# A two-block transformer kernel: the first normalisation by token tiles, wide and narrow matmuls in runs of sixteen, and another order in the mLSTM

## What is computed

```python
# first block, after its four mixers and their gates
mixed = jnp.sum(gates * y, axis=2) @ w_mix_out[l]
x = layer_norm(DEEPNORM_ALPHA * x + mixed, ln_mix_g[l], ln_mix_b[l])   # the first normalisation, "x1"
xa = cross_attention(x, mem_n, xattn_q[l], xattn_k[l], xattn_v[l], xattn_o[l])
x = layer_norm(DEEPNORM_ALPHA * x + xa, ln_x_g[l], ln_x_b[l])          # "x2"
ff = conv_ffn(x, ffn_in[l], ...); x = layer_norm(DEEPNORM_ALPHA * x + ff, ...)

# second block
y_m = mlstm_mixer(q_m, k_m, v_m, o_m, i_m, f_m, conv_w, conv_b, gate_b, mh_g)  # four heads
y_a = dilated_attention(q_a, k_a, v_a, rel_bias)
y = jnp.concatenate([y_m, y_a], axis=-1) @ w_out[l]; x = layer_norm_2(...)
y = memory_cross_attention(x, mem, xq, xk, xv, xo);  x = layer_norm_2(...)     # "x4", "x5"
y = (jax.nn.silu(x @ w1) * (x @ w3)) @ w2;           x = layer_norm_2(...)
```

## Time and profile before

| | |
|---|---|
| median of three runs | 3334.51 us |
| the profiled execution | 3333.03 us |
| its span, first to last instruction | 3331.1 us |
| PE busy | 3271.8 us (98%) |
| DVE busy | 1998.8 us (60%) |
| ACT busy | 1351.2 us (41%) |
| mean granted clock of PE | 0.993 of full speed |
| 16 DMA engines, mean rate | 191 GB/s |

### The profile page before, as it was taken

The page is one execution under the profiler, slowest core; times in us unless marked ns, Lnnn a source line. Parts: engine busy times, 40 slices in busy tenths (PEclk is TensorE's granted clock), DMA queues, the critical chain, the costliest instruction groups (busy, mean ns, idle before and its releaser), DMA issues.

```text
span 3331.1 us, 43422 instructions
## 1 busy us (share of the span) xinstructions
PE 3271.8 (98%) x18557; PEld 2850.6 (86%) x18557; DVE 1998.8 (60%) x1622; ACT 1351.2 (41%) x898; POOL 0.2 (0%) x4
## 2 busy tenths in 40 slices
PE   8999999999989999999999999999999999999998
PEld 8988888887878888888888889799998988888886
DVE  6455666757677666675565675774456644444556
ACT  4333555433335444443333433343333444444332
POOL 0000000000000000000000000000000000000000
PEclk9999999999999999999999999999999999999999
DMA  7744456678536555555646455655545555555553
GB/s 259 218 153 164 173 190 227 216 246 298 165 118 207 197 176 181 197 191 197 217 162 207 157 172 187 208 203 173 169 152 202 193 186 189 189 176 196 195 189 139
DMA packets 309424, 635.60 MB, mean 191 GB/s; under 512 B 10888, under 2 KB 16820, under 8 KB 307124
## 3 DMA queue, kind: packets, MB, share of 16 engines
q1 hardware_dynamic: 296080, 587.50, 52.3%
q10 hardware_dynamic: 13220, 46.25, 3.8%
HBM read 618.51 MB, written 15.20 MB: 190 GB/s over the span
## 4 chain that ended last, share of the span: by engine, by line
PE 89%; DVE 6%; ACT 2%; issue 2%; DMA 1%; ACTq 0%; SPq 0%; DVEq 0%
PE ps L961 40%; PE ps L1026 34%; PE ps L956 14%; ACT whi L570 1%; DVE wlo L1487 1%; PE ps L1030 1%; DMA wraw<-in_w_in 1%; DVE l_a L2148 1%; DVE m_t L1540 0%; DVE alt_l L1540 0%; DVE tok L1697 0%; DVE tok L1702 0%; DVE tok L1540 0%; DVE tok L2325 0%; DVE tok L2324 0%
## 5 line engine op out<-in xcount | busy, mean ns | idle before, releaser
L1487 DVE TENSOR_TENSOR wlo<-wraw,whi 128x2048 fp32r<-128x2048 f32 x549 | 1244.8, 2279 | 756.1 <-ACT whi L570 746.9
L570 ACT ACTIVATE whi<-wraw 128x2048 fp32r<-128x2048 f32 x549 | 1041.9, 1906 | 1424.2 <-PE ps L961 637.7
L1026 PE MATMUL ps<-act_hl,whi 128*128 128x512 f32 (+1 forms) x2976 | 787.4, 384 | 0.0
L961 PE MATMUL ps<-whi,act_hl 128*128 128x512 f32 x2128 | 661.8, 392 | 0.7 <-DVE wlo L1487 0.7
L1026 PEld LDWEIGHTS ps<-act_hl,whi 128*128 128x128 f32 x2976 | 502.3, 188 | 62.6
L1026 PEld LDWEIGHTS ps<-act_hl,wlo 128*128 128x128 f32 x2832 | 438.5, 188 | 57.7
L961 PEld LDWEIGHTS ps<-whi,act_hl 128*128 128x128 f32 x2128 | 396.3, 188 | 83.4 <-issue 1.9
L1026 PE MATMUL ps<-act_hl,wlo 128*128 128x256 f32 x2832 | 463.0, 281 | 0.0
L956 PE MATMUL ps<-act_hl,whi 128*128 128x256 f32 (+1 forms) x2400 | 441.0, 286 | 5.4 <-DVE wlo L1540 4.1
L961 PE MATMUL ps<-wlo,act_hl 128*128 128x512 f32 x1064 | 414.4, 389 | 0.0
L956 PEld LDWEIGHTS ps<-act_hl,whi 128*128 128x128 f32 (+1 forms) x2400 | 376.6, 193 | 8.0 <-issue 5.5
(11 more groups left out here) (322 smaller groups left out, 2443.1 us busy)
## 6 DMA issues: line engine op xcount, KB each, us to landing
wraw<-in_w_in SPq DMA_DIRECT2D x156, 1024.0 KB, 5.2
wraw<-in_w SPq DMA_DIRECT2D x132, 1024.0 KB, 5.2
wraw<-in_ffn_in SPq DMA_DIRECT2D x88, 1024.0 KB, 5.0
wraw<-in_ffn_out SPq DMA_DIRECT2D x44, 1024.0 KB, 5.1
wraw<-in_w_branch SPq DMA_DIRECT2D x16, 1024.0 KB, 5.2
wraw<-in_w_mix_out SPq DMA_DIRECT2D x16, 1024.0 KB, 5.5
wraw<-in_w_out SPq DMA_DIRECT2D x16, 1024.0 KB, 5.4
wraw<-in_xk SPq DMA_DIRECT2D x16, 1024.0 KB, 5.2
```

Of the source, the lines that this page charges most:

```text
L570: act.activation(whi[:, slot, k, c], wraw[:, slot, k, c], ACT.Copy).then_inc(hi_done, 1)
L961: ins = pe.matmul(o, x, wk, start=first and n == 0, stop=stop and n == 2, skip_group_check=True)
L1026: return pe.matmul(o, left, right, start=start, stop=stop, skip_group_check=True)
L1487: dve.tensor_tensor(wlo[:, slot, k, c], wraw[:, slot, k, c], whi[:, slot, k, c].bitcast(F32), ALU.subtract).then_inc(lo_done, 1)
```

## The change

1. `double`: PE waits for the high part of the unit alone, does the sixteen wide matmuls of all four chunks, waits for the low part, and does the sixteen narrow ones. Before, the two kinds alternated in fours.
2. x1 joins the normalisations by token tiles. The last of the mixing product's four columns is made by `last_column` (until now written out for x5 alone), the nine matmuls on constants go, and `gate_apart` makes the queries in two passes: its first pass takes the first token tile with the high weights, its second the second tile and the low weights. Its result is two halves side by side, so that ACT copies one of them out of PSUM first and DVE then adds the other one to it, where DVE copied before. ACT's work on units is redistributed: `hi(13)`, three inside `norm_apart`, `hi(3)`, that copy, `hi(1)`. DVE takes the last quarter's residual from `x_again` tile by tile, and the second tile's sum is put ahead of the scaling of the first tile's last quarter.
3. mLSTM: the convolution of q for the second pair of heads moves to the end of the first pair, between the last hand-over to PE and the wait for its answer, with `ahead[0] = 0`, and ACT does its SiLU there, behind `hi(2)`. The scaling of k goes ahead of the sigmoid's hand-over. The wait for the small load goes down to where the gains are used.

```diff
-        APART = ("x2", "x5")
+        APART = ("x1", "x2", "x5")
@@ ScalarE
-            hi(16)
-            norm(act_h)
+            hi(13)
+            norm_apart(act_h)
             act.wait_ge(unit_done, BASE["xq"])
             gains_for("x2")
-            hi(4)
+            hi(3)
+            act.wait_ge(unit_done, BASE["xq"] + 4)
+            both = ps[:, 0:2048].rearrange("p (s two t) -> p s two t", s=CB, two=2)
+            act.activation(x_s[1][:, :, :], both[:, :, 1, :], ACT.Copy).then_inc(half_saved, 1)
+            hi(1)
...
-                mapping((q[:, :, :], l_a[:, :, :], ACT.Silu))
+                if g == 0:
+                    mapping((q[:, :, :], l_a[:, :, :], ACT.Silu))
...
                 hi(2)
+                if g == 0:
+                    mapping((l_in[1][0][:, :, :], l_a[:, :, :], ACT.Silu))
@@ TensorE, double
-                    pe.wait_ge(lo_done, w.at("unit"))
+                    n = w.at("unit")
+                    pe.wait_ge(hi_done, n)
                     slot = (w.n["unit"] - 1) % SLOTS
                     for k in range(CB):
                         for s in range(CB):
                             mm(... whi ..., hi[:, CB * u + k, :, :], u + k == 0, False)
+                    pe.wait_ge(lo_done, n)
+                    for k in range(CB):
                         for s in range(CB):
                             x = mm(... wlo ..., hi[:, CB * u + k, 0, :], False, ...)
@@ TensorE
+            def last_column(name, hi, lo):
+                w.at("block")
+                products(T_BLOCK, 1, hi, lo, PC, last=False)
+                first = w.now("unit") + 1
+                for u in range(3):
+                    pe.wait_ge(lo_done, first + u)
+                    x = tile_unit(first + u, 0, hi, lo, PC, CB * (u + 1), False, u == 2)
+                x.then_inc(tile_done, 1)
+                for u in range(3):
+                    if u == 2:
+                        flip_tile(name, 0)
+                        flip_tile(name, 1)
+                    tile_unit(w.at("unit"), 1, hi, lo, PC, CB * (u + 1), False, u == 2).then_inc(unit_done, 1)
...
-            stay_warm(PC, 9)
-            column(first_of="x1", turning=("x1", EARLY))
+            last_column("x1", alt_h, alt_l)
+            w.at("block")
+            gate_apart("x1")
@@ VectorE
-            residuals(x_again, (4, 4, 4, 4), 147)
-            ahead[0] = 147
-            norm("x1", tok, act_h, act_l, (0, 0, 148, 0))
+            residuals(x_again, (4, 4, 4), 144)
+            lo_to(145)
+            dve.wait_ge(tile_done, w.at("tile"))
+            link(tile_sum(3, 0, PC, x_again))
+            tile_statistics(3, 0)
+            ahead[0] = 0
+            tile_deviation(0)
+            dve.wait_ge(gains_in, gains_loaded("x1"))
+            tile_normal("x1", 0, (0, 1))
+            tile_normal("x1", 0, (2,))
+            tile_low("x1", act_h, act_l, 0)
+            tile_low("x1", act_h, act_l, 1)
+            dve.wait_ge(unit_done, w.at("unit", 4))
+            w.at("block")
+            kept(tile_sum(3, 1, PC, x_again))
+            tile_normal("x1", 0, (3,))
+            tile_statistics(3, 1)
+            second_tile("x1", 145)
             lo_to(151)
-            kept(copy(x_q[:, :, :], four(arrived(4))))
+            dve.wait_ge(unit_done, w.at("unit", 4))
+            w.at("block")
+            dve.wait_ge(half_saved, w.at("half"))
+            both = ps[:, 0:2048].rearrange("p (s two t) -> p s two t", s=CB, two=2)
+            kept(tt(x_q[:, :, :], both[:, :, 0, :], x_s[1][:, :, :], ALU.add))
@@ VectorE, mLSTM, g in 0, 1
-                dve.wait_ge(small_in, 16 * SMALL[f"ml{g}"])
                 fill(behind_lstm, LSTM_FILL[g][0])
-                for part, x in enumerate((q, k)):
-                    ...
+                if g == 0:
+                    convolved(0, 0)
+                convolved(g, 1)
                 ahead[0] = at_unit[0] + 1
-                to_act(copy(st[:, 16:17], ident[:, 0:1]))
                 to_pe(dve.tensor_scalar(k[:, :, :], k[:, :, :], 1.0 / 16, None, ALU.mult))
+                to_act(copy(st[:, 16:17], ident[:, 0:1]))
...
+                    dve.wait_ge(small_in, 16 * SMALL[f"ml{g}"])
                     link(tt(l_h[:, :], l_h[:, :], l_norm[:, :], ALU.mult))
                     to_pe(tt(l_h[:, :], l_h[:, :], o[:, qt, :], ALU.mult))
                     if qt:
                         lo_to(at_unit[0] + 2)
+                        if g == 0:
+                            ahead[0] = 0
+                            convolved(1, 0)
                     from_pe()
```

More of the change, by code:

```diff
@@ L1216, in _ @@
             flip("mixed", 2)
+            def last_column(name, hi, lo):
[11 more added lines that the diff above has]
+                    tile_unit(w.at("unit"), 1, hi, lo, PC, CB * (u + 1), False, u == 2).then_inc(unit_done, 1)
             def square(hi, lo, first_of, turning=None):
                 column(T_BLOCK, hi=hi, lo=lo, first_of=first_of, turning=turning)
-                column(T_BLOCK, hi=hi, lo=lo)
                 column(T_BLOCK, hi=hi, lo=lo)
@@ L1458, in _ @@
             column(T_BLOCK)
[L1459 to L1470, removed]
+            last_column("x5", act_h, act_l)
             ffn("x5", by_tiles=True)
@@ L1677, in norm, with tile_sum @@
                     low(name, hi, dst, q)
-            def tile_sum(cb, h, bank):
+            def tile_sum(cb, h, bank, from_=tok):
                 o = bank + h * UNIT
-                return dve.scalar_tensor_tensor(tok[:, cb, h, :], tok[:, cb, h, :], ALPHA, ps[:, o:o + UNIT], ALU.mult, ALU.add)
+                return dve.scalar_tensor_tensor(tok[:, cb, h, :], from_[:, cb, h, :], ALPHA, ps[:, o:o + UNIT], ALU.mult, ALU.add)
             def tile_statistics(cb, h):
@@ L2131, in _, with convolved, tap @@
             dve.wait_ge(kept_out, 16)
+            def convolved(g, part):
+                x, r = l_in[g][part], part * 8 + 4 * g
+                def tap(j, c):
+                    return col(f"c2w{j}", r + c)
+                for c in range(4):
+                    dve.tensor_scalar(l_a[:, c, :], x[:, c, :], tap(3, c), col("cb2", r + c), ALU.mult, ALU.add
+                                      ).then_inc(dve_step, 1)
+                dve.wait_ge(dve_step, w.at("step", 4))
+                for j, s in ((2, 1), (1, 2), (0, 3)):
+                    for c in range(4):
+                        y = dve.scalar_tensor_tensor(l_a[:, c, s:T], x[:, c, 0:T - s], tap(j, c), l_a[:, c, s:T],
+                                                     ALU.mult, ALU.add)
+                        if j == 0 and c == 3:
+                            to_act(y)
+                        else:
+                            y.then_inc(dve_step, 1)
+                    dve.wait_ge(dve_step, w.at("step", 4 if j else 3))
@@ L2155, in _ @@
+                if g == 0:
+                    convolved(0, 0)
+                convolved(g, 1)
                 ahead[0] = at_unit[0] + 1
+                to_pe(dve.tensor_scalar(k[:, :, :], k[:, :, :], 1.0 / 16, None, ALU.mult))
                 to_act(copy(st[:, 16:17], ident[:, 0:1]))
-                to_pe(dve.tensor_scalar(k[:, :, :], k[:, :, :], 1.0 / 16, None, ALU.mult))
                 for qt in range(NT):
```

## The result

| | before | after |
|---|---|---|
| median of the runs | 3333.88 us (five, 3332.65 to 3334.53) | 3315.43 us (five, 3314.37 to 3316.11) |
| profiled execution | 3333.03 us, span 3331.1 | 3314.37 us, span 3312.6 |
| mean granted clock there | 0.993 | 0.996 |

The account below looks back on a forecast made before the run. PE, busy 98% of the span, was taken as the bound. Savings of 7.8 + 5.7 + 6.6 = 20.1 us from 3333.03 gave 3312.9, and 1.5 more for the median 3314.4 us; range 3309.5 to 3320.5.

Parts of the forecast that it names:

- The step that mattered: Gate and up units: narrow to wide costs 0.027 us, the way back gives 0.007; 5.567 instead of 5.613 a unit.
- order is neutral: Rival for the gate and up units: matmul order is worth nothing, total 3322.2 us; chance 0.07.
- The wait drains PE: Rival for the units: narrow matmuls start only when the last wide one has left, 37 us, 3351; chance 0.03.
- Last column to scores: Mixing product's last column to cross-attention scores: 53.8 instead of 60.1 us, 6.3 less.
- PE's wait at the second tile's first flip: First normalisation: PE's wait of 0.54 us in the third normalisation grows here, to near 1.9.
- all 1.36 us: First normalisation: everything for the second tile comes 1.36 us later, as its sum precedes the first tile's last scaling.
- the piece from the last matmul of the queries to the scores: End of the first normalisation: at least 2.5 us, at most 4.4, taken as 3.4.
- from bias to turning: Second mLSTM pair: PE's next turning 15.6 us behind the bias, at 1964.2 instead of 1970.79, 6.6 less.
- the wait there: Second mLSTM pair: a new PE wait of about 1.5 us at its next turning behind the bias.
- The last low part of the cover: Fourth cover unit before the second mLSTM pair: ready at 1942.6 as PE begins it; up to 0.5 us, taken as 0.
- 0.6 us for a low stretch at the scores: Cross-attention scores: idle piece of some 3.2 us may bring a lower clock; charged 0.6, from 0 to 4.
- The rival in which the idle piece costs more clock: Rival at the scores: a low stretch of 10.24 us costs 5 instead of 0.6, total 3319; chance 0.08.

Follow-up runs that it names:

- order alone: Kernel before, with sixteen wide then sixteen narrow matmuls a unit behind the one old wait for the low part; 3325.55 us.
- waits alone: Kernel before, order kept in fours, PE awaiting the high part at the unit's start and the low part before the first narrow matmul; 3336.78 us.
- runs of eight: Changed kernel with eight wide, eight narrow, then the same again in each unit, instead of sixteens; 3315.0 us in one execution.
- turned units: Changed kernel with each second unit doing its narrow matmuls first, then the wide ones; median of four 3312.63 us.
- shortened kernel: Changed kernel; first normalisation scales half of the last quarter during DVE's wait and makes the third low part behind the queries' sum; 3314.57 us.
- part 2 alone: Kernel before with only the first normalisation by token tiles; 3328.6 us, ten runs.
- both together: Changed kernel with each second unit narrow first and the two shortened places of the first normalisation; median of five 3311.63 us.
- part 3 alone: Kernel before with only the mLSTM change (convolution of q moved, k scaled earlier, gains awaited later); 3327.83 us, ten runs.
- scaled k alone: Kernel before with only the scaling of k put ahead of the sigmoid's hand-over; 3331.03 us in one execution.

## Why the prediction was right

*Part 1.* Forecast 5.567 us a unit and 7.8 in all; measured 5.567 and twice 3.92 in the 84-unit stretches. The step that mattered was to compare each kind of matmul with its own and to charge the difference to the change from narrow to wide. The order alone and the waits alone separate it from the wait, and the kernels with runs of eight and with turned units put it on the number of changes. The rival "order is neutral" is refuted. By the Trainium skill's gap (TensorE: Matmul & The Clock Gate, Back-to-back issue gap), which that section gives for an isolated matmul, a reservation that the prediction left out, all four orders would take the same time, since the formula knows only the columns. The traces disagree, 5.613 to 5.557 us for the same 32 matmuls. "The wait drains PE" is refuted too: 0.00 us a unit where it needed 0.12.

*Part 2.* Last column to scores forecast 53.8, measured 53.75. Its pieces: PE's wait at the second tile's first flip forecast 1.9, measured 1.68, because I let all 1.36 us pass through; the piece from the last matmul of the queries to the scores forecast 3.4 between bounds of 2.5 and 4.4, measured 3.48 from the start of that matmul and 3.36 from its end slot 0.12 later, from which the forecast counted. The taken value was a choice between the ends, and the shortened kernel shows what set it: the third low part. With it out of the way the piece is 2.72 from the start and 2.60 counted as the forecast did, close to the lower bound. That the stage came out at 53.8 is shown; that the gain of 6.3 came out too may have luck in it, as the paragraph on the clock says.

*Part 3.* Forecast 15.6 us from bias to turning, measured 15.69; the wait there forecast 1.5, read as 1.09 from the end of the last matmul and 1.37 from its start. The last low part of the cover, called level between the two engines, made PE 0.1 late, inside the 0 to 0.5. I credited the step to the convolution's move and the scaling together; it is the move alone. The 6.6 holds for the kernel before as it was profiled, with 10.24 us of low clock here; against kernels with less of it the same part gives 5.8 to 6.3.

*The clock.* This is the term that was mis-sized. I charged 0.6 us for a low stretch at the scores, and 0 everywhere else. In this trace there was none at the scores, and one in each of three places that the change leaves alone, +1.2, +0.8 (1.0 less the 0.2 of the first pair) and +1.2 us, with 1.1 won at the start (1.6 by the clock, less the 0.5 of the longer wait at 612.08): a net 2.1 us where 0.6 was charged. That these steps are the clock's is read from where the stretches lie, not from a run that took them away. The forecast of 3312.9 for the trace was 1.5 under the 3314.37 measured; the median was taken 1.5 above the trace and lay 1.1 above it, so that the forecast median of 3314.4 was only 1.0 under the measured one. The rival in which the idle piece costs more clock has something in it: the low stretch at the scores came in four of the six kernels with part 2 (part 2 alone, units turned round, the shortened normalisation, and both together), and in none of the six without it, at 1.64 us in the first of them where it was priced at 5. What decides whether it comes I didn't find. The profiled kernel before had such stretches as well: behind the mixing product, at 902.96, one cost it 1.25 us of the 60.1, as the kernel with the order alone shows, which had none there and took 58.84 us; the one with part 3 alone took as long. Their first normalisation is the old one, idle places and all, so the stretch isn't part of it each time: four of the six kernels without part 2 have it, and none of the six with part 2. Whether the shorter idle places keep it away isn't shown. Against a kernel without it part 2 gives 5.1 us and not 6.3, near the 5.3 of the medians. Those 5.1 are the removed matmuls and the overlap of the tiles; the two weren't separated in runs.

## What to carry over

Where matmuls of two widths feed the same products and PE never waits, put equal widths together, price it from the trace by the distances right behind a change of width, and multiply by the number of changes. When a wait goes, name the next thing on each engine that is late, not only on the one that waited; the scaled k alone traded 5.06 us of waiting for 2.82. Leave one to two us of doubt for each place where the clock may fall: here the forecast stages held to about 0.1 us at full clock, and each low stretch that came or went on work of PE's moved the total by 0.9 to 1.6 us. A low stretch can also lie in the trace that you start from, and then part of a gain read against it may be luck: look for one in each stage, and compare with another kernel in which that stage is unchanged.

## What the runs showed of the hardware

- A wide matmul (512 columns) behind narrow ones (256) starts its successors late: in the changed kernel's unit 0.233, 0.236, 0.228, 0.233 and 0.231 us, then 0.227 on. I had not expected that the stretches of 84 units agree to 0.01 us, in both feed-forwards and between kernels: 471.52 in all six with fours, 467.60 in all three with sixteens, 466.79 in both with turned units.
- PE's wait for a signal long given, in the midst of matmuls, costs nothing: 471.52 us with 84 such waits more, and without.
- A stretch at the lower level stood at PE's wait of some 5 us for k in all four kernels that have it (10.2 us long in the kernel before, 6.8 in the order alone, the waits alone and part 2 alone), one of 3.4 us at the wait of 2.82 in the kernel with the scaling alone, and none there in any of the seven kernels with the convolution moved.
- What a low stretch costs depends on what it falls on: 3.4 us of it on scores of the cross-attention or on units cost 0.9 to 1.6 us, and nearly nothing on matmuls on constants ahead of a wait (1718.7 in the kernel before).
- The lower clock level also comes and goes without any change to the code around it. The same instructions in kernels that differ elsewhere had them or had not: at 977 to 985 us in the changed kernel, in the one with the waits and in part 2 alone (+1.20, +1.24, +1.21 us), and not in the kernel before or the one with the order alone. Executions of one program differ by as much, 3309.57 to 3314.5 us in the fastest.
